# Modulation slabs summed into one PSUM bank, with one copy and one set of folds per layer part

## The chip, the cores and the metric

The kernel runs on one core of a Trainium2 chip. The metric is the device time of one execution in microseconds (us). The kernel before takes 2806.68 us, the median of three runs (2805.99 to 2807.84).

The engines are named as the profile names them: PE (TensorE, matrix products; PEld are its weight loads), DVE (VectorE), ACT (ScalarE), POOL (GpSimd) and SP (SyncE, which here only issues DMAs).

## The reference, cut to what matters

Two layers. In each, a vector `c` of 1024 (and its counterpart `c_ctx` for the context rows) is passed through silu and multiplied by a matrix of 1024 x 6144. The 6144 results are six groups of 1024, by which the activations are shifted, scaled and gated.

```
silu_c = jax.nn.silu(c)
silu_cc = jax.nn.silu(c_ctx)
for i in range(DEPTH):
    mod = (silu_c @ w_ada[i] + b_ada[i])[:, None, :]
    mod_c = silu_cc @ w_ada[i] + b_ada[i]
    sh1, sc1, g1, sh2, sc2, g2 = jnp.split(mod, 6, axis=-1)
    ...
    u = _layer_norm(x) * (1.0 + sc1) + sh1
    uc = _layer_norm(xc) * (1.0 + sc1c) + sh1c
    f, fc = _token_mixer(u, uc, w_in[i], ...)
    x = _post_norm(DEEPNORM_ALPHA * x + g1 * f, ln1_g[i], ln1_b[i])
    u2 = _layer_norm(x) * (1.0 + sc2) + sh2
    ...
    m = _moe(...)
    x = _post_norm(DEEPNORM_ALPHA * x + g2 * m, ln2_g[i], ln2_b[i])
```

The mixer (a state space part with a convolution, a Fourier part and gates) and the mixture of 64 experts are the rest of the kernel. All is float32.

## The kernel before, in words

The kernel is written with explicit engine programs and semaphores. Each engine runs its own list in the order in which the code emits it, and waits where a `wait_ge` says so. No scheduler stands behind it.

**Where the modulation is computed.** The 6144 columns of a layer's `w_ada` come in two parts. The first 2048 (shift and scale of the mixer's input) are four wide slabs of 512 columns. PE works on them at the very start of the kernel for layer 0, and between the experts of layer 0 and the summing of their results for layer 1. The other 4096 are 16 late slabs of 256 columns. They ride in the weight ring of a mixer call (call 0 for layer 0, call 3 for layer 1), one behind each of the call's first 4 + 10 + 2 slabs of `w_in`: the four `four` slabs, the ten `xbc` slabs (convolution channels) and two of the six `z` slabs. The `dt` slab between `four` and `xbc` has 48 columns and no late slab. The ring has four slots. SP loads slab n when the product of slab n - 4 is done.

**A slab's products** (`fourth_products`, L663). `csil` holds silu(c) and silu(c_ctx) as columns 0 and 1 of 32, the other 30 being zero; the contraction of 1024 is 8 steps of 128. Step k writes to partitions 32 (k % 4) onwards, so four partial sums of two rows each lie in four groups of 32 partitions of one bank. ACT copies that bank to SBUF (L1198 wide, L1254 late), with two buffers.

**A fold** (`fold`, L670) brings the sums into the layout in which they are used, one modulation column a partition, and adds the four parts: for each 128 columns of the copy, a matmul with the copy as weights and `fold4` as the moving operand, a constant of 128 x 2 with ones where partition % 32 is 0 or 1. A wide slab needs four such matmuls and a late slab two. PE does the fold of slab n - 1 behind the products of slab n (L690 wide, L791 late), and the last slab's behind the last (L692 wide, L844 late, the latter behind the third `z` slab).

**Use.** DVE adds the bias to the folded sums in one instruction and 1 to the scales in another (`modulate`, L1479), for the wide part in `first_modulations` (L1496) and for the late part after the state passes (L1615). For layer 1, `first_modulations` stands in the middle of DVE's combining of the expert results (L2030), and PE goes from the last wide fold to summing these results (`sum_results`, L643), whose input POOL gathers with plain DMAs (L2116). The second gather waits for the third wide product, the third for the fourth (L2113).

**The xbc loop.** Per slab, PE does 16 matmuls of 256 columns (L747), the late slab's 8 (L667), a fold and four transposes of an older slab (L775). ACT starts the convolution (L1271), DVE does four taps (L1558), ACT the silu (L1238) and the copy of the transposed tile (L1245). Behind the loop DVE waits for ACT's exponentials (L1573) and weights the input of the state products (L1582), which PE awaits at L715.

Each float32 matmul leaves two records in the trace, so x16 there is 8 matmuls.

## Time and profile before

| | |
|---|---|
| time, median of 3 runs | 2806.68 us (2805.99 to 2807.84) |
| profiled execution: span | 2806.5 us |
| its own time | the page gives none beside the span; the median of the runs is 0.2 us above it |
| PE busy | 2563.5 us (91%) |
| DVE / ACT / POOL busy | 962.5 / 543.0 / 238.5 us |
| ACT: copy of a late slab (L1254, 32 of them) | 0.38 us each |
| mean granted clock of PE | 0.957 of full speed |
| late slabs in the trace | 56 to 206 us (layer 0), 1735 to 1890 us (layer 1) |
| wide slabs in the trace | 14 to 40 us (layer 0), 1572 to 1586 us (layer 1) |

The groups of instructions by line give the number of records, the busy time and the mean of one, and behind the bar the engine's idle time just before them with what ended it. The timeline gives start, duration, engine, line and operation, and in brackets the idle time before a row and its releaser, where there was any. A row that merges several instructions runs from the first one's start to the last one's end, so the start of the next row says more on what a step costs than the duration, since matmuls are pipelined.

### The profile page before, as it was taken

Reading aid. Unit: us, or ns where it says so; the run is one execution under the profiler, and the core shown is the slowest. Engines: PE = TensorE matmul, PEld = TensorE weight load, DVE = VectorE, ACT = ScalarE, POOL = GpSimd, SP = SyncE. Lnnn points to the kernel's source line nnn. Section 1 sums busy time; section 2 is a strip of 40 time slices with the busy share of each in tenths; the row PEclk is TensorE's granted clock in tenths of the full one; section 3 lists DMA queues with packets and bytes.
Section 4 is the critical chain, followed back from the end, with each engine's and each line's share of the span. In section 5 each row is a group of like instructions: output and inputs, shape, how many; then the busy total and the mean of one; then the engine's idle time right before and its main releaser. Section 6 shows DMA issues by size and latency. Waiting matters only on the chain. (4 is left out here: it accounts for less than half of the span.)

```text
span 2806.5 us, 35244 instructions
## 1 busy us (share of the span) xinstructions
PE 2563.5 (91%) x11348; PEld 1623.7 (58%) x11348; DVE 962.5 (34%) x2255; ACT 543.0 (19%) x1210; POOL 238.5 (8%) x394
## 2 busy tenths in 40 slices
PE   6999999999997899999999889999997899999994
PEld 3878888887873343433443367878885333434441
DVE  1335724448166111111111375444705311111114
ACT  1233511325131111111111012233411111111110
POOL 0000000000000111112111100000000112112110
PEclk8999999999998999999999989999998999999998
DMA  8764444445335999999999744764441899999993
GB/s 292 237 198 148 158 143 138 135 140 161 120 125 197 410 407 407 408 394 412 408 405 409 295 165 132 227 203 150 147 157 55 343 398 391 390 387 401 381 364 145
DMA packets 293119, 742.43 MB, mean 265 GB/s; under 512 B 33176, under 2 KB 208416, under 8 KB 238240
## 3 DMA queue, kind: packets, MB, share of 16 engines
q1 hardware_dynamic: 264672, 665.59, 63.7%
q0 software_dynamic: 28352, 75.56, 6.9%
q8 instruction: 61, 1.00, 0.1%
q14 instruction: 34, 0.28, 0.0%
HBM read 734.60 MB, written 52.58 MB: 280 GB/s over the span
## 5 line engine op out<-in xcount | busy, mean ns | idle before, releaser
L747 PE MATMUL psum<-arena 128*128 128x256 f32 x1984 | 455.1, 389 | 8.9 <-ACT arena L1212 5.0
L1116 PE MATMUL psum<-arena 128*64 128x512 f32 x1472 | 367.9, 645 | 83.6 <-DMA arena<-in_w 80.6
L747 PEld LDWEIGHTS psum<-arena 128*128 128x128 f32 x1984 | 385.2, 196 | 67.0 <-issue 5.7
L980 PE MATMUL psum<-arena 128*128 128x512 f32 x832 | 374.8, 594 | 0.0
L2004 DVE COPY arena<-psum 128x512 f32<-128x512 f32 x92 | 63.6, 691 | 612.8 <-PE psum L992 308.7
L1116 PEld LDWEIGHTS psum<-arena 128*64 128x64 f32 x1472 | 114.3, 147 | 270.0 <-issue 261.8
L1431 ACT ACTIVATE arena<-psum 128x512 f32<-128x512 f32 x92 | 55.0, 598 | 1057.6 <-PE psum L992 595.3
L758 PE MATMUL psum<-arena 128*128 128x256 f32 (+1 forms) x1088 | 239.6, 379 | 5.0 <-ACT arena L1212 5.0
L980 PEld LDWEIGHTS psum<-arena 128*128 128x128 f32 x832 | 152.2, 192 | 154.3 <-issue 154.3
L758 PEld LDWEIGHTS psum<-arena 128*128 128x128 f32 x1088 | 204.7, 199 | 38.3 <-ACT arena L1212 5.2
L992 PE MATMUL psum<-arena 128*128 128x512 f32 x416 | 198.5, 621 | 12.9 <-DVE arena L1809 9.7
L1558 DVE SCALAR_TENSOR_TENSOR grow<-psum,par,grow 128x255 f32<-128x255 f32 (+1 forms) x304 | 136.2, 479 | 153.9 <-ACT grow L1271 148.4
L907 PE MATMUL psum<-arena 128*128 128x256 f32 x768 | 173.2, 379 | 0.0
L2100 POOL DMA_INDIRECT results<-arena,ids x92 | 93.1, 1012 | 923.8 <-DVE arena L2004 923.8
L1145 PE MATMUL psum<-arena 128*64 128x512 f32 x736 | 168.1, 599 | 0.0
L2001 DVE COPY arena<-psum 128x256 f32<-128x256 f32 x92 | 39.0, 424 | 374.3 <-PE psum L987 374.3
L907 PEld LDWEIGHTS psum<-arena 128*128 128x128 f32 x768 | 144.2, 190 | 23.0
L992 PEld LDWEIGHTS psum<-arena 128*128 128x128 f32 x416 | 77.2, 195 | 128.2 <-issue 115.9
L1102 PEld LDWEIGHTS psum<-cst,arena 128*128 128x128 f32 x736 | 92.8, 193 | 69.4 <-issue 66.9
L2054 POOL MEMSET arena<- 128x1024 f32 x4 | 3.7, 950 | 1378.4 <-DVE arena L1800 1378.4
L1145 PEld LDWEIGHTS psum<-arena 128*64 128x64 f32 x736 | 48.6, 137 | 113.8 <-issue 113.8
L1102 PE MATMUL psum<-cst,arena 128*128 128x128 f32 x736 | 102.7, 283 | 8.6 <-DVEq L1975 4.5
(305 smaller groups left out, 2454.8 us busy)
## 6 DMA issues: line engine op xcount, KB each, us to landing
arena<-in_w SPq DMA_DIRECT2D x414, 1024.0 KB, 14.6
arena<-in_w_in SPq DMA_DIRECT2D x92, 1024.0 KB, 5.3
arena<-in_w_ada SPq DMA_DIRECT2D x32, 1024.0 KB, 7.8
arena<-results POOLq DMA_DIRECT2D x12, 2048.0 KB, 9.5
arena<-in_w_br_ssm SPq DMA_DIRECT2D x24, 768.0 KB, 4.4
arena<-in_w_ada SPq DMA_DIRECT2D x8, 2048.0 KB, 15.3
arena<-cumulated SPq DMA_DIRECT2D x36, 384.0 KB, 4.3
arena<-in_w_br_four SPq DMA_DIRECT2D x12, 1024.0 KB, 5.2
```

The costliest lines, as they stand in the source:

```text
L747: last = mm(o[:, a, :], w[:, k, a * P:(a + 1) * P], rhs[:, k, :], start=k == 0, stop=k == ks - 1, skip_group_check=True)
L758: last = mm(o[:, a, 0:cols], lhs[:, k, a * P:(a + 1) * P], w[:, k, 0:cols], start=k == 0, stop=k == KD - 1, skip_group_check=True)
L907: last = mm(o[:, a, :], w[:, k, a * P:(a + 1) * P], rhs[:, k, :], start=k == 0, stop=k == KD - 1, skip_group_check=True)
L980: last = mm(o.rearrange("p (a n) -> p a n", a=2), lhs(k), w[:, k, :, :], start=k == 0, stop=k == KD - 1)
L992: last = mm(bank[5 + half][:, :], src[:, k, :], w[:, k, half * 512:(half + 1) * 512], start=k == 0, stop=k == 1)
L1102: last = tp(psum[:, 2 + k // 4, (k % 4) * P:(k % 4 + 1) * P], xg[b].rearrange("p (q k) -> p k q", k=KD)[:, k, :], ident)
L1116: last = mm(bank[0][c, :].rearrange("p (a n) -> p a n", a=2), xTe[0][:, k, c], w13[b][:, k, :, :], start=k == 0, stop=k == KD - 1)
L1145: last = mm(bank[5 + half][c, :], hT[0][:, k, c], w2s[b][:, k, half * 512:(half + 1) * 512], start=k == 0, stop=k == 1)
L1431: a_(ysb[b][:, 0:512], bank[5], ACT.Copy).then_inc(z["y_act"], 1)
L1558: i_ = V.scalar_tensor_tensor(dst, src[:, a * SEQ + lo + sh:a * SEQ + hi + sh], par[:, 60 + tap * 20 + ch:61 + tap * 20 + ch], dst, ALU.mu ...
L2004: V.tensor_copy(ysb[b][:, 512:1024], bank[6]).then_inc(z["y_dve"], 1)
L2100: gp.indirect_dma_start(scratch["y"][l], bass.IndirectOffsetOnAxis(ap=ids[:, q:q + 1], axis=0), ysb[b], None, bounds_check=last_row, oob_i ...
```

## The change

- `csil` becomes 62 columns wide with the two silu columns at 30 and 31 and zeros around them. Slab j takes the 32 columns from 2 (15 - j) on, so that its two rows land at rows 2j and 2j + 1 of each group of 32 partitions, and its products add zeros to the other rows.
- All wide slabs of a layer add up in bank 0 and all late slabs in bank 3. Only the very first products of a part start the sum, and only the last ones end it.
- ACT copies the bank once per part, behind the last slab. PE folds once per part, with 8 columns (wide) or all 32 (late) of a wider `fold4`.
- PE no longer waits for ACT's copies between slabs. The second buffer of the copies goes.
- The folded sums now lie with the 128-column block as the outer index and the slab as the inner one, so `modulate` takes one strided addition per block: four for the wide part and two for the late one.
- What is computed, the slabs, their loads and the order of these in SP's queue stay.

```diff
-    pack[:, C_SEL:C_SEL + 2] = (p[:, None] % 32) == np.arange(2)
+    pack[:, C_SEL:C_SEL + 32] = (p[:, None] % 32) == np.arange(32)
...
-        fold4 = cst[:, C_SEL:C_SEL + 2]
+        fold4 = cst[:, C_SEL:C_SEL + 32]
-        csil = sb("csil", [P, KD, 32])
+        csil = sb("csil", [P, KD, 2 * ADA_LATE + 30])
-        late_part = [arena[:, seg_at + b * SW:seg_at + (b + 1) * SW] for b in range(2)]
+        late_part = arena[:, seg_at:seg_at + SW]
-        wide_part = {l: [arena[:, part_at[l] + b * ADA_W:part_at[l] + (b + 1) * ADA_W] for b in range(2)] for l in range(DEPTH)}
+        wide_part = {l: arena[:, part_at[l]:part_at[l] + ADA_W] for l in range(DEPTH)}
...
 
-                def fourth_products(o, w):
-
+                def fourth_products(o, w, j, n):
+
+                    lo = 2 * (ADA_LATE - 1 - j)
                     for k in range(KD):
                         q = 32 * (k % 4)
-                        i_ = mm(o[q:q + 32, :], csil[:, k, :], w[:, k, :], start=k < 4, stop=k >= 4)
+                        i_ = mm(o[q:q + 32, :], csil[:, k, lo:lo + 32], w[:, k, :], start=j == 0 and k < 4, stop=j == n - 1 and k >= 4,
+                                skip_group_check=True)
                     return i_
 
-                def fold(o, part, n):
+                def fold(o, part, n, w):
 
                     for c in range(n):
-                        i_ = mm(o[:, 2 * c:2 * c + 2], part[:, c * P:(c + 1) * P], fold4, start=True, stop=True)
+                        i_ = mm(o[:, w * c:w * (c + 1)], part[:, c * P:(c + 1) * P], fold4[:, 0:w], start=True, stop=True)
                     i_.then_inc(s_ada_tp, 1)
-
-                def wide_fold(j):
-                    pe.wait_ge(s_ada_row, part_no(l, j) + 1)
-                    fold(bank[2][:, 8 * j:8 * j + 8], wide_part[l][j % 2], 4)
 
                 for j in range(ADA_WIDE[l]):
                     r = ADA_RING[l]
                     pe.wait_ge(s_ada[j % r], 16 * (j // r + 1) + 16 * l)
-                    if j >= 2:
-                        pe.wait_ge(s_ada_row, part_no(l, j - 2) + 1)
-                    fourth_products(bank[j % 2], wide[l][j % r]).then_inc(s_ada_mm, 1)
+                    fourth_products(bank[0], wide[l][j % r], j, ADA_WIDE[l]).then_inc(s_ada_mm, 1)
                     if j == 1:
                         pe.wait_ge(s_par, 16 * 7 * (l + 1))
                         tp(bank[7][:, 0:60], praw[0:60, 0, :], ident[0:60, 0:60])
                         tp(bank[7][:, 60:180], praw[0:120, 1, :], ident[0:120, 0:120]).then_inc(s_tp_par, 1)
-                    if j:
-                        wide_fold(j - 1)
-                wide_fold(ADA_WIDE[l] - 1)
+                pe.wait_ge(s_ada_row, 2 * l + 1)
+                fold(bank[2], wide_part[l], ADA_W // P, 2 * ADA_WIDE[l])
                 if l:
                     sum_results(l - 1)
 
...
                         last.then_inc(t_ctp.sem, 1)
 
-                    def late_fold(n):
-                        pe.wait_ge(s_ada_row, late_no(l, n) + 1)
-                        fold(bank[6][:, 4 * n:4 * n + 4], late_part[n % 2], 2)
+                    def late_fold():
+                        pe.wait_ge(s_ada_row, 2 * l + 2)
+                        fold(bank[6], late_part, SW // P, 2 * ADA_LATE)
 
                     def late_ada(kind, j):
                         n = ada_after(m, kind, j)
...
                             return
                         no = SLAB_NO[(m, "ada", n)]
                         pe.wait_ge(s_slab_in[no % NSLOT], 16 * (no // NSLOT + 1))
-                        if n >= 2:
-                            pe.wait_ge(s_ada_row, late_no(l, n) - 1)
-                        fourth_products(bank[3 + n % 2][:, 0:SW], ring[no % NSLOT]).then_inc(s_slab, 1)
-                        if n:
-                            late_fold(n - 1)
+                        fourth_products(bank[3][:, 0:SW], ring[no % NSLOT], n, ADA_LATE).then_inc(s_slab, 1)
 
                     if full:
                         for j in range(4):
@@ -841,7 +823,7 @@
                             late_ada("z", j)
                             state_products(m, True, 3 * j + 2, 3 * j + 3)
                             if m in LATE_CALLS and j == 2:
-                                late_fold(ADA_LATE - 1)
+                                late_fold()
                         scores_product(0)
 
                         def feature_dft(g):
...
             act.wait_ge(s_csil, 1)
             for v in range(2):
-                last = a_(csil[:, :, v], craw[:, v, :], ACT.Silu)
+                last = a_(csil[:, :, 2 * ADA_LATE - 2 + v], craw[:, v, :], ACT.Silu)
             last.then_inc(s_csil, 1)
             for l in range(DEPTH):
                 for j in range(ADA_WIDE[l]):
-                    act.wait_ge(s_ada_mm, wide_no(l, j) + 1)
-                    if j >= 2:
-                        act.wait_ge(s_ada_tp, sums_before(l) + j - 1)
-                    a_(wide_part[l][j % 2], bank[j % 2], ACT.Copy).then_inc(s_ada_row, 1)
+                    if j == ADA_WIDE[l] - 1:
+                        act.wait_ge(s_ada_mm, wide_no(l, j) + 1)
+                        a_(wide_part[l], bank[0], ACT.Copy).then_inc(s_ada_row, 1)
                     if j == 1:
                         act.wait_ge(s_tp_par, l + 1)
...
                     def late_copy(kind, j):
-                        n = ada_after(m, kind, j)
-                        if n is None:
+                        if ada_after(m, kind, j) != ADA_LATE - 1:
                             return
-                        act.wait_ge(s_slab, SLAB_NO[(m, "ada", n)] + 1)
-                        if n >= 2:
-                            act.wait_ge(s_ada_tp, late_no(l, n) - 1)
-                        a_(late_part[n % 2], bank[3 + n % 2][:, 0:SW], ACT.Copy).then_inc(s_ada_row, 1)
+                        act.wait_ge(s_slab, SLAB_NO[(m, "ada", ADA_LATE - 1)] + 1)
+                        a_(late_part, bank[3][:, 0:SW], ACT.Copy).then_inc(s_ada_row, 1)
 
                     if full:
...
                 inverse_root(mv[:, 1:2], 1.0)
                 return V.scalar_tensor_tensor(xres[:, t, :], tmp, rsq[:, 3:4], lnrow[:, 1, :], ALU.mult, ALU.add)
 
-            def modulate(lo, hi, src):
-
-                link(V.tensor_tensor(modc[:, lo:hi, :], src.rearrange("p (j v) -> p j v", v=2),
-                                     par[:, lo:hi].unsqueeze(2).to_broadcast([P, hi - lo, 2]), ALU.add))
+            def modulate(lo, hi, src, wide_by):
+
+                n = (hi - lo) // wide_by
+                for c in range(wide_by):
+                    last = V.tensor_tensor(modc[:, lo + c:hi:wide_by, :], src[:, 2 * n * c:2 * n * (c + 1)].rearrange("p (j v) -> p j v", v=2),
+                                           par[:, lo + c:hi:wide_by].unsqueeze(2).to_broadcast([P, n, 2]), ALU.add)
+                link(last)
                 plain = [o for o in (8, 32) if lo <= o < hi]
...
             def first_modulations(l):
                 dve.wait_ge(s_parc, 2 * l + 2)
-                dve.wait_ge(s_ada_tp, sums_before(l) + ADA_WIDE[l])
+                dve.wait_ge(s_ada_tp, 2 * l + 1)
                 hi = 4 * ADA_WIDE[l]
-                modulate(0, hi, bank[2][:, 0:2 * hi])
+                modulate(0, hi, bank[2][:, 0:2 * hi], ADA_W // P)
                 dve.wait_ge(s_modc, 2 * l + 1)
 
...
                     state_pass(rounds, 0)
 
                     if m in LATE_CALLS:
-                        dve.wait_ge(s_ada_tp, late_no(l, ADA_LATE))
-                        modulate(16, 48, bank[6][:, 0:4 * ADA_LATE])
+                        dve.wait_ge(s_ada_tp, 2 * l + 2)
+                        modulate(16, 48, bank[6][:, 0:4 * ADA_LATE], SW // P)
                         dve.wait_ge(s_modc, 2 * l + 2)
 
 
```

**PE, start of the program (wide slabs of layer 0).** L667 and L659 are the products, L673 and L666 the folds, L688/L689 and L675/L676 transposes of parameters, L721 and L707 the transposes of the normalized input. Before:

```order
L667 MATMUL psum<-arena,csil 32x512 x16
L688 MATMUL psum<-cst,praw 128x60
L689 MATMUL psum<-cst,praw 128x120
L673 MATMUL psum<-cst,arena 128x2 x4
L667 MATMUL psum<-arena,csil 32x512 x8
L673 MATMUL psum<-cst,arena 128x2 x4
L667 MATMUL psum<-arena,csil 32x512 x8
L673 MATMUL psum<-cst,arena 128x2 x8
L721 MATMUL psum<-cst,arena 128x128 x16
```

Of the change, the same place on PE:

```order
L659 MATMUL psum<-arena,csil 32x512 x16
L675 MATMUL psum<-cst,praw 128x60
L676 MATMUL psum<-cst,praw 128x120
L659 MATMUL psum<-arena,csil 32x512 x16
L666 MATMUL psum<-cst,arena 128x8 x4
L707 MATMUL psum<-cst,arena 128x128 x16
```

Sixteen fold matmuls become four, and nothing stands between the products of the last two slabs.

**PE, two turns of the xbc loop (call 0).** L747 and L733 are the slab's matmuls, L667 and L659 the late slab's, L775 and L761 the transposes. Before:

```order
L747 MATMUL psum<-arena 128x256 x16
L667 MATMUL psum<-arena,csil 32x256 x8
L673 MATMUL psum<-cst,arena 128x2 x2
L775 MATMUL psum<-cst,arena 128x128 x4
L747 MATMUL psum<-arena 128x256 x16
L667 MATMUL psum<-arena,csil 32x256 x8
L673 MATMUL psum<-cst,arena 128x2 x2
L775 MATMUL psum<-cst,arena 128x128 x4
```

Of the change, two turns at the same place on PE:

```order
L733 MATMUL psum<-arena 128x256 x16
L659 MATMUL psum<-arena,csil 32x256 x8
L761 MATMUL psum<-cst,arena 128x128 x4
L733 MATMUL psum<-arena 128x256 x16
L659 MATMUL psum<-arena,csil 32x256 x8
L761 MATMUL psum<-cst,arena 128x128 x4
```

The two fold matmuls of each turn are gone, and nothing else changes its place.

## Rows read from the trace of the kernel before

**Rows 1.** The page of the profile: span.
```profile
span 2806.5 us, 35244 instructions
```

**Rows 2.** Timeline of layer 0, two late slabs: start, duration, engine, line.
```profile
56.26 1.07 PE L667 MATMUL psum<-arena,csil 128*32 128x256 f32 x16
57.26 7.17 PE L747 MATMUL psum<-arena 128*128 128x256 f32 x32
...
64.36 1.07 PE L667 MATMUL psum<-arena,csil 128*32 128x256 f32 x16
...
65.36 0.61 PE L673 MATMUL psum<-cst,arena 128*128 128x2 f32 x4
...
65.83 7.15 PE L747 MATMUL psum<-arena 128*128 128x256 f32 x32
```

**Rows 3.** Groups by line, PE, 56.2 to 182 us, then 1734.5 to 1866 us.
```profile
L747 PE MATMUL psum<-arena 128*128 128x256 f32 x417 | 95.6, 388 | 0.0
...
L673 PE MATMUL psum<-cst,arena 128*128 128x2 f32 x52 | 7.9, 256 | 0.0
...
L673 PE MATMUL psum<-cst,arena 128*128 128x2 f32 x52 | 7.9, 257 | 0.0
```

**Rows 4.** Timeline of PE, layer 0, behind the first z slab.
```profile
195.93 0.61 PE L673 MATMUL psum<-cst,arena 128*128 128x2 f32 x4
...
196.40 0.89 PE L715 MATMUL psum<-arena 128*128 128x384 f32 x2
```

**Rows 5.** Timeline of PE and DVE at the xbc loop's end, layer 0.
```profile
167.69 1.07 PE L667 MATMUL psum<-arena,csil 128*32 128x256 f32 x16
...
176.63 1.07 PE L667 MATMUL psum<-arena,csil 128*32 128x256 f32 x16
...
184.79 0.26 DVE L1573 TENSOR_TENSOR arena<-arena 128x96 f32<-128x96 f32 x1 [2.42 <-ACT arena L1290]
...
185.76 1.65 PE L715 MATMUL psum<-arena 128*128 128x384 f32 x2 [2.26 <-DVE arena L1582]
```

**Rows 6.** Timeline of layer 0 behind the last wide slab's products.
```profile
37.71 2.13 PE L673 MATMUL psum<-cst,arena 128*128 128x2 f32 x16
37.83 0.60 ACT L1198 ACTIVATE arena<-psum 128x512 f32<-128x512 f32 x1 [6.27 <-PE psum L667]
...
39.95 0.19 DVE L1481 TENSOR_TENSOR modc<-psum,par 128x32 f32<-128x32 f32 x1 [14.92 <-PE psum L673]
...
46.62 9.71 PE L747 MATMUL psum<-arena 128*128 128x256 f32 x32 [4.96 <-ACT arena L1212]
```

**Rows 7.** Timeline of layer 1, last wide folds and start of the summing.
```profile
1584.41 1.95 PE L673 MATMUL psum<-cst,arena 128*128 128x2 f32 x16
...
1586.17 0.53 POOL L2116 DMA_DIRECT2D arena<-results  x1 [3.63 <-DMA arena<-results]
1586.22 20.85 PE L655 MATMUL psum<-arena 128*128 128x512 f32 x48
...
1596.88 1.28 DVE L2021 TENSOR_TENSOR arena<-arena,psum 128x512 f32<-128x512 f32 x2 [3.64 <-PE psum L655]
```

**Rows 8.** Windows (after ACT and POOL: PEclk), and timeline at the dt products.
```profile
36.00:38.00 2.00, 2.00 (x14) 0.34 (x6) 0.00 (x0) 0.17 (x1) 0.00 (x0) 0.50 1.10 350
90.00:92.00 2.00, 2.00 (x6) 1.55 (x6) 1.72 (x9) 0.00 (x0) 0.00 (x0) 0.50 1.10 355
...
82.93 4.33 PE L758 MATMUL psum<-arena 128*128 128x48 f32 x32
87.07 9.95 PE L747 MATMUL psum<-arena 128*128 128x256 f32 x32
...
1773.02 8.37 PE L747 MATMUL psum<-arena 128*128 128x256 f32 x32
```

**Rows 9.** One line's instructions, L1481 and L667: ns as min/median/max, starts.
```profile
L1481 DVE TENSOR_TENSOR modc<-psum,par x4: 191/203/225, 40.0 to 1899.5; 128x32 f32<-128x32 f32 x2, 128x64 f32<-128x64 f32 x2
...
L667 PEld LDWEIGHTS psum<-arena,csil x640: 105/110/178, 14.2 to 1889.0; 128*32 128x32 f32 x160
```

More of the change, by code:

```diff
@@ L49 @@
 C_SEL = C_TRI8 + NGRP * NGRP
-C_STEP = C_SEL + 2
+C_STEP = C_SEL + 32
 C_FOLD = C_STEP + P
@@ L423, in wide_no @@
             return j + (ADA_WIDE[0] if l else 0)
-        def part_no(l, j):
-            return j + (ADA_WIDE[0] + ADA_LATE if l else 0)
-        def sums_before(l):
-            return ADA_WIDE[0] + ADA_LATE if l else 0
-        def late_no(l, n):
-            return sums_before(l) + ADA_WIDE[l] + n
         @block.sync
```

## The prediction

> **What bounds the kernel now.** I read the page first: one core, span 2806.5 us [rows 1], and TensorE (PE) is busy for most of it. A share of the whole span does not say what an edit is worth in one stretch, so next came the groups of instructions by line over the two stretches in which the late slabs of the modulation run, 56.2 to 182 us (layer 0) and 1734.5 to 1866 us (layer 1) [rows 3]. The reader is to see the last column there: no group of PE has idle time before it, in either stretch. So here PE is the bound, and every instruction that leaves PE's queue moves what follows forward. Third came the timeline of PE, to read what one fold costs in place [rows 2, 4]; fourth the end of the xbc loop, where PE does wait [rows 5]; last the two places where the wide slabs run [rows 6, 7] and the granted clock [rows 8].
>
> **The change part by part**
>
> **Folds inside the late stages (removed).** A late slab without a fold behind it starts its products at 56.26, and the next slab's matmuls start at 57.26: 1.00 us. With a fold pair: 64.36, fold at 65.36, next slab at 65.83 [rows 2]. The products take the same 1.00 us, the pair adds 65.83 - 65.36 = 0.47 us. It costs the same in the z part (195.93 to 196.40) [rows 4]. Each layer has 15 such pairs inside the stage (13 of them in each stretch of rows 3, 52 records at 4 a pair, and 2 among the z slabs), and one behind the stage, which stays.
>
> Of the 15, one saves nothing: the pair behind the last xbc slab. PE's later wait there ends on a chain that starts with the slab product, not with the fold: the product is done at 176.6, VectorE's convolution, ScalarE's exponentials (VectorE waits 2.42 us for them at 184.79) and VectorE's weighting follow, and PE idles 2.26 us before 185.76 [rows 5]. Take the fold out and that pause is 0.47 us longer. So 14 pairs a layer, 28 in all, each 0.47: 28 x 0.47 = -13.2 us. This is the term that carries the forecast.
>
> **The one fold that stays** has 32 columns in place of 2 (8 in place of 2 for the wide slabs). No row shows that form. From below it is the fold of today, 0.47/2 = 0.23 us a matmul; from above the 48-column matmuls of the dt product, 82.93 to 87.07 for 16, 0.26 us each [rows 8]. Two matmuls a layer: 0 to +0.06 us each time. I take 0.
>
> **Copies on ScalarE (removed):** 15 a layer of 0.38 us. ScalarE waits for PE or VectorE in the loop, and in the tail the wait is for VectorE's convolution, which does not wait for the copy. 0 us; at best -0.4 us a layer if the copy is in the chain of rows 5 after all.
>
> **Wide slabs of layer 0.** The folds of slabs 0 to 2 lie between loads that PE waits for, so they are hidden now. At the end the last two folds run back to back from 37.71, and the copy of the last slab (37.83, 0.60 long) is done at 38.43; the second fold starts after the first, at about 38.77 (half of the row's 2.13 us). Afterwards the single fold starts when the copy is done: 0.3 us earlier. The addition on VectorE (39.95) becomes four, each on 8 elements a partition. A row of this line lasts 191 to 225 ns [rows 9], so the three more are 0 to 0.68 us; not chained, they overlap, and I take 0.3. ScalarE and then PE (46.62, after 4.96 us of waiting) hang on this chain [rows 6], so the sum counts: -0.3 + 0.3 = 0, bounds -0.3 to +0.5.
>
> **Wide slabs of layer 1.** Three sets of four folds leave PE, about 1.0 us each, and behind the last products PE waits for the 0.6 us copy. PE would be ready for the summing of results some 2 us earlier than 1586.22. But the gather of the results that it sums landed only then: GpSimd, which waits for the same landing, was released at 1586.17 [rows 7]. So this gain is hidden by a transfer. The second gather is released by the third wide product, about 0.9 us earlier than now, and shares the DMA with the first: the first could land up to 0.9 us later. From 1596.88 on VectorE's chain carries the stage, and it now has the three further additions, +0.3. I take +0.3; bounds -2.0 (the landing is no limit) to +1.6 (0.9 later and 0.68 of VectorE).
>
> **The late modulation** is two additions in place of one, in a stretch in which VectorE waits for PE. 0. The larger zero-padded tile and the 30 further constant columns (15 KB) load while PE waits for the first slabs. 0, at most 0.1.
>
> **Clock of PE.** Behind the dt product of layer 0 the same 16 matmuls take 9.95 us instead of 7.15, with the clock at 1.2 GHz (0.50 in the row of 90 to 92 us); in layer 1 8.37 us [rows 8]. The engine had done 48-column matmuls just before it fell. The fall costs 2.80 and 1.22 us, so the same work can cost either, by how it lies in time, and the change moves it. I take the present sum of the two, 4.0; bounds -2.8 (one gone, the other at 1.2) to +1.6 (both as dear as 2.8).
> The Trainium skill ("TensorE: Matmul & The Clock Gate", section "HAM oscillation") says that bursts of matmuls with waits between them fall back to the slow clock. By that rule this edit has a price: the folds fill pauses in the wide stages, and without them PE is idle more. The trace agrees where PE waits long for a slab: in the row of 36 to 38 us, behind the wait for the last wide one, the clock is 0.50 [rows 8]. By the rule the sum below would be up to 4.4 us higher, the first rival; without it, it stands as it is.
>
> **Sum.** -13.2 + 0 + 0.3 + 0 = -12.9 us. Against the profiled execution: 2806.5 - 12.9 = 2793.6 us. The median of the three runs, 2806.68, is 0.2 above that span, so 2793.8 us. Everything behind the two stages (expert loads included) starts from what PE, VectorE or ScalarE have finished, so I see nothing that takes the gain back.
>
> **Rivals**
>
> 1. **The clock turns against it.** Without the folds PE pauses 0.7 us and more in the layer 1 wide stage, and a fall of the clock lands in the summing of results, which is on the path [rows 7], and the dt product's falls become the dear kind. Price by rows 8: one more fall 2.8, the layer 1 one dearer by 1.6: +4.4, 2798.2 us. For: behind both dt products of these stretches the matmuls are slow [rows 8]. Against: most of the removed work is inside a dense stretch, where it is the fold that is the thin part. Its mirror image is as possible: one dt fall gone and the other cheap (-2.8), and the summing in layer 1 1 us earlier, 2790.0 us.
> 2. **The xbc loop is bound by the convolution, not PE**, and only the folds among the four-slabs and z slabs count: 3 + 2 a layer, 10 x 0.47 = 4.7, 2802 us. For: VectorE and ScalarE work in every xbc turn. Against: no idle time before any PE group [rows 3].
> 3. **Slower: the loads of the shifted slices.** Each load will take its 32 words a partition from an offset that moves by 8 bytes a slab, not from the start of a packed block of 32. The load takes 110 ns now [rows 9], 16 of them in a slab's 1.00 us. If the new pattern makes each 50 ns longer and none of it hides, 32 late slabs cost 32 x 16 x 0.05 = 25.6 us, less 12.9 saved: 2819.4 us. It decides from 25 ns a load (12.9 / 512). For: the offset has no row in this trace. Against: 128 adjacent bytes a partition are read in both, and a slab has time left beside its loads (16 x 0.11 = 1.76 us of them pass in its 1.00 us, so they overlap already).
> 4. **The gain is given back** behind the stage, at a transfer that does not start from PE's progress. I found none; 2800 us if one takes half.
>
> **How the numbers follow.** Forecast as summed 0.68; rival 1 against 0.09 and its mirror image 0.13; rival 2 0.04; rival 3 0.03; rival 4 0.03. The forecast's own bounds, not all at one end, give 2791 to 2797; with the clock's two sides the range is 2789.3 to 2798.5, which leaves out rivals 2 to 4 and the tails of rival 1 and its mirror, under 2 in 10. What a measurement can tell here is 0.2%, 5.6 us. Faster by more: forecast, rival 1 and mirror, rival 4, 0.93; within: rival 2, 0.04; slower: rival 3, 0.03.
>
> **What would show it.** Right: 24 records in place of 192 on the fold's line (2 a matmul, 4 + 2 matmuls a layer); a turn of the xbc loop of 8.47 in place of 8.94 us (167.69 to 176.63) [rows 5]; still no idle before PE's groups in both stretches; the pause before 185.76 of today 2.7 instead of 2.26 us; the summing in layer 1 beginning within 0.1 us of a landing of results, as now. Wrong: a slab's products longer than 1.00 us (rival 3), idle time of PE before the convolution's transposes (rival 2), or the matmuls behind the dt product at a time other than 8.4 to 10 us (the clock).

## The result, and the profile after

The changed kernel takes 2783.7 us in the median of four runs (2783.04 to 2787.53), against 2806.34 us for the kernel before in the same comparison (2798.96 to 2807.84). The ratio is 0.9923, with a 95% interval of 0.9905 to 0.9940: 22.6 us faster. The forecast was 2793.8 us with a range of 2789.3 to 2798.5. The direction was right, the size was not: 1.8 times the forecast gain of 12.9 us, and below the range.

All comparisons below also give means. Runs of one kernel scatter with a standard deviation of some 4 us (the kernel before: 2798.2 to 2814.5 over 50 further runs, mean 2806.4; the changed kernel: mean 2783.8 ± 0.9 over 8), so a single execution can't tell 5 us.

First the page of the changed kernel: the span, and the busy time of each engine.

```profile
span 2781.6 us, 34816 instructions
PE 2529.3 (91%) x11180; PEld 1595.5 (57%) x11180; DVE 963.5 (35%) x2263; ACT 527.9 (19%) x1174; POOL 238.7 (9%) x394
```

The span is 24.9 us shorter than in [rows 1]. Next the groups of PE by line, 46 to 173.5 us, which answer to [rows 3]: records, busy us, mean ns, idle time before them.

```profile
L733 PE MATMUL psum<-arena 128*128 128x256 f32 x448 | 102.0, 387 | 4.1 <-ACT arena L1193 4.1
L659 PE MATMUL psum<-arena,csil 128*32 128x256 f32 x224 | 15.0, 385 | 0.0
L761 PE MATMUL psum<-cst,arena 128*128 128x128 f32 x32 | 5.2, 286 | 0.0
```

The fold's group is gone from the stretch, and PE still idles before none of the loop's groups (the 4.1 us of L733 are before its first matmul at 47.43, outside the stretch of [rows 3]). PE remains the bound. Timeline of PE at two late slabs, to be read beside [rows 2]: start, duration, line.

```profile
56.84 1.07 PE L659 MATMUL psum<-arena,csil 128*32 128x256 f32 x16
57.84 7.17 PE L733 MATMUL psum<-arena 128*128 128x256 f32 x32
64.94 1.07 PE L659 MATMUL psum<-arena,csil 128*32 128x256 f32 x16
65.94 2.42 PE L733 MATMUL psum<-arena 128*128 128x256 f32 x10
```

The next slab's matmuls start 1.00 us behind a late slab's products, every time, with no fold between. The two lines that the change rewrote, durations as min/median/max in ns:

```profile
L659 PEld LDWEIGHTS psum<-arena,csil x640: 105/110/178, 13.3 to 1862.0; 128*32 128x32 f32 x160
L666 PE MATMUL psum<-cst,arena x24: 192/276/379, 37.9 to 1871.8; 128*128 128x8 f32 x16, 128*128 128x32 f32 x8
L1461 DVE TENSOR_TENSOR modc<-psum,par x12: 154/161/192, 39.9 to 1872.2; 128x8 f32<-128x8 f32 x8, 128x32 f32<-128x32 f32 x4
```

The weight loads from the shifted slices take what they took [rows 9], 105/110/178. The folds are 24 records.

What the forecast did not have is at the dt product of layer 0. Timeline of PE there, and two windows (after the busy times of PE, PEld, DVE, ACT and POOL stands PEclk, the granted clock); both answer to [rows 8].

```profile
82.15 3.77 PE L744 MATMUL psum<-arena 128*128 128x48 f32 x32
85.76 7.14 PE L733 MATMUL psum<-arena 128*128 128x256 f32 x32
...
90.00:92.00 2.00, 2.00 (x11) 1.77 (x10) 1.72 (x9) 0.00 (x0) 0.00 (x0) 1.00 1.12 372
86.00:88.00 2.00, 2.00 (x11) 1.74 (x11) 1.55 (x5) 0.28 (x1) 0.00 (x0) 1.00 1.03 343
```

Before, the 48-column product took 4.14 us from its start to the next, and the 32 records behind it 9.87 us to the next line (96.94), with a granted clock of 0.50 (1.2 GHz) for more than half of it. Now it is 3.61 and 7.07 us (to 92.83), at 1.00 (2.4 GHz). So the prediction's own sign of being wrong (these records at a time other than 8.4 to 10 us) is there. It is the same in layer 1, where the row of 32 records took 8.37 us and now takes 7.14:

```profile
1748.10 3.77 PE L744 MATMUL psum<-arena 128*128 128x48 f32 x32
1751.71 7.14 PE L733 MATMUL psum<-arena 128*128 128x256 f32 x32
1758.78 1.07 PE L659 MATMUL psum<-arena,csil 128*32 128x256 f32 x16
```

To see where all of it comes from, I lined up the starts of PE's groups in both traces and noted where the difference changes. Each row is a start before, a start after, and their difference:

| what lies up to there | before | after | difference |
|---|---|---|---|
| first weights of call 0 | 46.62 | 47.43 | +0.8 |
| four slabs, dt product and the 32 records behind it | 98.4 | 93.8 | -4.6 (clock -3.6, folds -1.8, beside the +0.8) |
| rest of the xbc loop, to its last transposes | 178.56 | 170.01 | -8.6 |
| first state products, early z slabs | 206.89 | 196.62 | -10.3 (clock -1.1, folds -0.9) |
| call 1 | 735.38 | 721.12 | -14.3 (clock -1.65 behind its dt product, -1.7 at its end) |
| experts of layer 0 (PE waits for weights), first two wide slabs of layer 1 | 1578.47 | 1561.52 | -17.0 (-0.8 of it clock, in the two slabs) |
| rest of the wide part of layer 1 | 1586.22 | 1568.25 | -18.0 |
| summing of the results, to the dt product of call 2 | 1636.79 | 1620.21 | -16.6 |
| call 2, and call 3 to the 32 records behind its dt product | 1782.79 | 1759.78 | -23.0 (folds -1.8, clock -1.7 at this dt product and -1.8 in call 2, where a pause is 1.1 shorter too) |
| late stage of layer 1 | 1862.47 | 1835.47 | -27.0 |
| end | | | -24.9 |

The folds show as 28 steps of 0.44 to 0.45 us (a turn of the xbc loop is 168.52 - 160.02 = 8.50, before 8.94 [rows 5]). That is 12.5 us. The rest, half of the gain, sits in other steps, and the largest that can be read one by one are those of the clock. The wide part of layer 1 does not carry it in this profile: the 1.0 us that it gains is gone when the summing ends.

Timeline of PE at the end of the xbc loop, which answers to [rows 5]:

```profile
168.52 1.07 PE L659 MATMUL psum<-arena,csil 128*32 128x256 f32 x16
169.52 0.66 PE L761 MATMUL psum<-cst,arena 128*128 128x128 f32 x4
...
174.76 0.30 PE L685 MATMUL psum<-cst,arena 128*32 128x128 f32 x1 [1.09 <-ACT arena L1226]
...
177.66 0.94 PE L701 MATMUL psum<-arena 128*128 128x384 f32 x2 [2.27 <-DVE arena L1563]
```

From the last late products to the first state product it is 9.14 us (168.52 to 177.66) and was 9.13 (176.63 to 185.76): the fold behind the last xbc slab saved nothing, as forecast, but the time it leaves appears ahead of the transposes at 174.76 and not in the last pause, which stays 2.27.

### The profile page after: what moved, and what is told of

Its sections match the earlier page's. It is cut to its first block and busy times, and to the rows that moved or that the text cites. A ratio compares the mean times of both kernels' runs of the same rounds, so it can differ in the third digit from the quotient of the medians.

```text
span 2781.6 us, 34816 instructions
## 1 busy us (share of the span) xinstructions
PE 2529.3 (91%) x11180; PEld 1595.5 (57%) x11180; DVE 963.5 (35%) x2263; ACT 527.9 (19%) x1174; POOL 238.7 (9%) x394
## 5 line engine op out<-in xcount | busy, mean ns | idle before, releaser
L733 PE MATMUL psum<-arena 128*128 128x256 f32 x1984 | 447.7, 385 | 6.9 <-ACT arena L1193 4.1
L1098 PE MATMUL psum<-arena 128*64 128x512 f32 x1472 | 361.2, 635 | 90.0 <-DMA arena<-in_w 88.2
L733 PEld LDWEIGHTS psum<-arena 128*128 128x128 f32 x1984 | 379.4, 193 | 66.4 <-issue 7.6
L974 PE MATMUL psum<-arena 128*128 128x512 f32 x416 | 198.5, 621 | 12.9 <-DVE arena L1790 9.7
L889 PE MATMUL psum<-arena 128*128 128x256 f32 x768 | 173.2, 379 | 0.0
L1127 PE MATMUL psum<-arena 128*64 128x512 f32 x736 | 168.1, 598 | 0.0
```

The lines of the kernel that those rows point to most:

```text
L733: last = mm(o[:, a, :], w[:, k, a * P:(a + 1) * P], rhs[:, k, :], start=k == 0, stop=k == ks - 1, skip_group_check=True)
L889: last = mm(o[:, a, :], w[:, k, a * P:(a + 1) * P], rhs[:, k, :], start=k == 0, stop=k == KD - 1, skip_group_check=True)
L974: last = mm(bank[5 + half][:, :], src[:, k, :], w[:, k, half * 512:(half + 1) * 512], start=k == 0, stop=k == 1)
L1098: last = mm(bank[0][c, :].rearrange("p (a n) -> p a n", a=2), xTe[0][:, k, c], w13[b][:, k, :, :], start=k == 0, stop=k == KD - 1)
L1127: last = mm(bank[5 + half][c, :], hT[0][:, k, c], w2s[b][:, k, half * 512:(half + 1) * 512], start=k == 0, stop=k == 1)
```

## The experiments

The columns: median, mean with its standard error, ratio to the kernel before on the same chip with 95% interval, and the time that TensorE's clock stood at 0.50 in the mixer stretches (60 to 810 and 1560 to 2090 us) of the one profiled execution.

| kernel | median | mean (runs) | ratio, interval | at 1.2 GHz |
|---|---|---|---|---|
| before | 2806.6 | 2806.4 ± 0.5 (50) | | 75 us |
| changed | 2783.7 | 2784.5 ± 1.0 (4) | 0.9923, 0.9905 to 0.9940 | 45 |
| changed, again | 2782.5 | 2783.2 ± 1.7 (4) | 0.9926, 0.9909 to 0.9943 | 48 |
| late_only | 2786.7 | 2787.0 ± 0.8 (4) | 0.9942, 0.9925 to 0.9958 | 48 |
| wide_only | 2800.9 | 2800.6 ± 1.2 (10) | 0.9986, 0.9975 to 0.9998 | 65 |
| refold | 2802.7 | 2802.3 ± 1.6 (10) | 0.9992, 0.9977 to 1.0007 | 58 |
| pair_at_dt | 2786.5 | 2784.8 ± 1.3 (5) | 0.9920, 0.9904 to 0.9936 | 51 |
| pairs_but_dt | 2796.3 | 2796.6 ± 2.1 (5) | 0.9957, 0.9941 to 0.9974 | 61 |
| wide_refold | 2784.6 | 2785.1 ± 0.8 (5) | 0.9921, 0.9906 to 0.9936 | 51 |
| fill | 2775.2 | 2775.9 ± 1.7 (4) | 0.9888, 0.9869 to 0.9908 | 31 |
| fill_before | 2798.3 | 2798.0 ± 0.8 (9) | 0.9970, 0.9958 to 0.9981 | 58 |
| hold_before | 2800.3 | 2799.9 ± 0.8 (12) | 0.9977, 0.9967 to 0.9987 | 34 |
| hold_wide | 2796.2 | 2796.7 ± 0.8 (8) | 0.9965, 0.9951 to 0.9978 | 31 |
| hold_after | 2786.7 | 2786.0 ± 0.9 (6) | 0.9930, 0.9915 to 0.9946 | 32 |

The last column is one execution each. The mean granted clock is on record for every execution, and since the traces show only the levels 0.50 and 1.00, twice what it lacks of 1, times the span, is an estimate of the time at 1.2 GHz in the whole execution: 234 ± 2 us before (50 executions), 212 ± 2 in the changed kernel (8), 228 ± 5 in `refold` (10), 203 ± 6 in `fill` (4), 212 ± 4 in `fill_before` (9), 188 ± 2 in `hold_before` (12), 199 ± 2 in `hold_after` (6). A microsecond at half speed costs at most 0.5, and less where TensorE waits. So the 21 us by which the changed kernel stands at 1.2 GHz for less time are worth up to 11 us, about what its gain has beside the folds.

### The changed kernel once more

No edit.

> The changed kernel again, beside the kernel before. Theory A (the folds give 28 x 0.45 = 12.5 us, and the other 10 to 12 us are falls of PE's clock that a shift in time happened to take away): the difference to before need not be the same on another chip or day, 2780 to 2792. Theory B (the other 10 us are work or waits that the change takes away, the same each time): 2783 to 2784 in every run.

Mean 2783.2 us, and again no fall of the clock behind the dt products of the two calls with late slabs. The extra gain is no accident of one comparison.

### The late part alone, the wide part alone

`late_only` has the shifted slices, one copy and one fold set for the 16 late slabs; the wide slabs are folded as before. `wide_only` is the reverse.

```
 late_only:  fourth_products(bank[j % 2], wide[l][j % r], 0, 1)      # wide slabs, each by itself
             fold(bank[2][:, 8 * j:8 * j + 8], wide_part[l][j % 2], 4, 2)
 wide_only:  fourth_products(bank[3 + n % 2][:, 0:SW], ring[no % NSLOT], 0, 1)   # late slabs, each by itself
             fold(bank[6][:, 4 * n:4 * n + 4], late_part[n % 2], 2, 2)
```

> Late slabs as in the change, wide slabs as before. Folds of the late part: 28 x 0.45 = 12.5 us less. Theory A: 2794 from the folds alone, and up to 10 us less where falls of the clock go with the shift; which falls go is read from the granted clock in the trace. Theory B, with the rest coming from the wide part: 2794, and wide_only then gives the other 10 us.

> Wide slabs as in the change, late slabs as before. By the steps of the prediction +0.3 us, 2806.6. Theory A: within 2 us of before, apart from falls of the clock that come or go. Theory B, with the rest from the wide part: 2796.

Against the mean before on that chip (2805.7), the late part gives 18.7 ± 1.2 us, though its folds are worth 12.5; the wide part gives 5.1 ± 1.5, forecast as nothing. With the late part alone the clock falls behind neither of these dt products. Timeline of PE of `late_only`, layer 0:

```profile
80.97 3.77 PE L760 MATMUL psum<-arena 128*128 128x48 f32 x32
84.58 7.14 PE L749 MATMUL psum<-arena 128*128 128x256 f32 x32
```

### The pairs of folds put back, without their waits

```
+                        if n:
+                            for c in range(2):
+                                mm(bank[6][:, 64 + 2 * c:66 + 2 * c], cst[:, c * P:(c + 1) * P], fold4[:, 0:2], start=True, stop=True)
```

The changed kernel with 15 pairs of matmuls a layer in the old form and place; they read a constant, wait for no copy, and nobody reads them.

> The change, with two fold matmuls put back behind each late slab from the second on (15 pairs a layer; they read a constant, wait for nothing and are not used). Copies and waits stay away. Theory A: PE's time is back, +12.5 us, and with it the old places in time: 2796 to 2808, with falls of the clock behind the dt products again. Theory B (copies, waits or the one bank gave the rest): 2796, with no more falls than in the changed kernel.

It costs 18.5 ± 1.9 us against the changed kernel's mean of 2783.8, where 30 pairs at 0.45 are 13.4, and 12.5 without the two behind the last xbc slabs, which fall into a pause. So the pairs as PE work alone, without copies or semaphores, take away more than their own duration. Timeline of PE of `refold` in layer 0; compare 3.77 in the changed kernel:

```profile
82.68 0.61 PE L777 MATMUL psum<-cst 128*128 128x2 f32 x4
83.14 4.78 PE L744 MATMUL psum<-arena 128*128 128x48 f32 x32
```

The product after the pair runs 4.58 us to the next line (87.72) instead of 3.61.

### Is it the pair beside the dt product?

The same three lines under `if n == 3:` (only the pair ahead of the dt product, one a layer) and under `if n and n != 3:` (all the others).

> The changed kernel with one fold pair put back per layer, behind the late slab that stands directly ahead of the dt product (it reads a constant and is not used). Theory A (thin work next to the dt product brings PE's clock down, and this pair tips it): the clock falls behind the dt product again, +3.3 us in layer 0 and +1.7 in layer 1 beside the pair's own 0.9: 2789.5. Theory B (a fall or none is where the dt product happens to lie in time): the pair costs its own 0.9 us, 2784.5, and any fall comes with about the chance it has elsewhere.

> The changed kernel with all pairs put back but the one of pair_at_dt (14 a layer). Theory A: no fall behind the dt products, 28 x 0.45 = 12.5 us more than the change: 2796. Theory B: 12.5 us and in addition falls as often as in the kernel with all 15, whose mean was 2802.4: 2801.

`pair_at_dt` costs 1.0 ± 1.6 us over the changed kernel; two pairs are 0.9 by themselves. In layer 0 the clock stays up with the pair in place, in layer 1 it falls. `pairs_but_dt` costs 12.8 ± 2.3, close to 28 x 0.45 = 12.6, although its profiled execution shows slow stretches behind both dt products without a pair ahead of them. Timelines of PE in layer 0, `pair_at_dt`, then `pairs_but_dt`:

```profile
83.53 0.61 PE L777 MATMUL psum<-cst 128*128 128x2 f32 x4
83.99 3.75 PE L744 MATMUL psum<-arena 128*128 128x48 f32 x32
```

```profile
81.29 4.06 PE L744 MATMUL psum<-arena 128*128 128x48 f32 x32
85.15 7.05 PE L733 MATMUL psum<-arena 128*128 128x256 f32 x25
```

The last row is cut off at the end of the window; the 32 records take 8.49 us to the next line (93.64).

So the simple theory, that the pair directly ahead of the 48-column product alone tips the clock, falls. In the one profiled execution of `pairs_but_dt` the falls are back without that pair, though its mean shows no cost beyond the pairs' own time. The two runs also show how far one profile and the mean can stand apart.

All profiles without fillers in the dt products, taken together, say more than any one of them. At the dt products of calls 0 and 3, the calls with late slabs, the clock falls in 7 of 8 cases with all pairs in place (`before`, `wide_only`, `refold`, `fill_before`), in both of `pairs_but_dt`, in one of two of `pair_at_dt`, and in 1 of 10 without pairs (the changed kernel twice, `late_only`, `wide_refold`, `fill`). Call 1 has no late slab, so nothing of the change is in it; there the clock falls in 4 of the 11 profiles (`before`, `pairs_but_dt`, `fill`, `fill_before`). In call 2 the whole dt product runs at 0.50 in all 11.

### Is the wide part's gain its folds?

```
+                    if j:
+                        for c in range(4):
+                            mm(bank[2][:, 64 + 2 * c:66 + 2 * c], cst[:, c * P:(c + 1) * P], fold4[:, 0:2], start=True, stop=True)
```

The changed kernel with the 12 wide folds a layer put back as dead work.

> The changed kernel with the three sets of four fold matmuls put back between the products of the wide slabs (they read a constant, wait for nothing and are not used). The two kernels with only the wide part changed or not changed say that the wide part gives 3 to 4.5 us in the mean. Theory A (PE's fold work ahead of the summing in layer 1 is what went): half or more of it comes back, 2785.5 to 2788. Theory B (the waits for the copies, or a changed load at the start): nothing comes back, 2783.8.

Mean 2785.1: +1.3 ± 1.2 us. That is within the error of nothing, and at most a part of the 3 to 5 us.

### Holding the clock up

`fill` is the changed kernel with matmuls that nobody reads, placed in pauses of PE: ahead of call 0's first product, and around the `heads_product` ahead of the state products.

```
+            def fill(o, n, cols):
+                for _ in range(n):
+                    mm(o[:, 0:cols], ident, cst[:, 0:cols], start=True, stop=True)
...
+                        if m == 0:
+                            fill(bank[1], 3, 512)
...
+                            if full:
+                                fill(bank[4], 2, 256)
                             if full:
                                 heads_product(m)
+                                fill(bank[4], 2, 512)
```

> The changed kernel with matmuls of a constant, not used, in PE's pauses: 3 of 512 columns while ScalarE writes the first u of layer 0, and 2 of 256 and 2 of 512 columns before the first state product of each call with all parts. If pauses are what lets the clock fall there, the long slow stretch at 35 to 52 us ends one step earlier (-1.7 us) and the three falls of 3.4 to 6.8 us ahead of the state products go (-1.7 to -3.4 each): 2776 to 2780. If not, or if the fillers come in the way, 2784 to 2786.

It is the fastest kernel of the study: mean 2775.9, 7.9 ± 1.9 us under the changed kernel. Its profile still has a fall of 3.4 us behind each dt product of layer 0 (83.1 to 86.5 in call 0, 455.2 to 458.6 in call 1). Timeline of PE of `fill`, layer 0, to be held against the rows of the changed kernel above:

```profile
174.35 1.98 PE L652 MATMUL psum<-cst 128*128 128x512 f32 x4
176.69 0.91 PE L708 MATMUL psum<-arena 128*128 128x384 f32 x2 [0.35 <-DVE arena L1572]
177.44 2.32 PE L753 MATMUL psum<-arena 128*128 128x256 f32 x10
```

PE's pause of 2.27 us is filled. From the last late products (167.55) to the state product it is 9.14 us, as in the changed kernel, and the ten records behind it take 2.15 us to the next line. In the changed kernel they took 3.84:

```profile
178.41 4.01 PE L744 MATMUL psum<-arena 128*128 128x256 f32 x10
182.25 0.81 PE L701 MATMUL psum<-arena 128*128 128x384 f32 x2
```

### The change measured again with the clock held

Four kernels test the cause: nearly the same fillers in the kernel before (`fill_before`, with bank 6 in place of bank 4 and four matmuls of 256 columns in place of two of 512), and in addition fillers inside the dt product of every call, in the kernel before (`hold_before`), in the wide part alone (`hold_wide`) and in the changed kernel (`hold_after`).

```
+                    def refill(done):
+                        if done % 8 == 0:
+                            fill(bank[6][:, 256:512], 3, 256)
-                    token_major("dt", 0, uT, 48)
+                    token_major("dt", 0, uT, 48, refill)
```

The dt product is 16 matmuls or 32 records; the fillers are 2 x 3 matmuls a call, which are 12 records of 0.223 us. The expectation of `hold_before` counts these records as matmuls, and the fall that it lists at 731 us is at the end of call 1 and not behind a dt product. That of `hold_after` overlooks the second fall in layer 0 of `fill`.

> The kernel before with the same filler matmuls as in the run 'fill' (3 of 512 columns while TensorE waits for the first transposed copies of call 0; 2 of 256 before and 4 of 256 after the heads product at the first state product of each full call; results never read). Theory C (the clock is the second half of the gain): the filler takes away the falls before the state products and leaves those behind the dt products, because the pairs of fold matmuls and the 48-column matmuls still stand there: 2806.9 - 8 = about 2799, and the difference to 'fill' (2775.9 in the mean) stays 20 to 25. Rival D (what the change gains beside the folds' own time is waits of the pairs and copies, not the clock): also 2799 and also 20 to 25; this run does not tell them apart by itself, it is the lower rung of 'hold_before'.

> As 'fill_before', and 3 filler matmuls of 256 columns behind every 8 of the 32 matmuls of each call's dt product (12 a call, 4 calls, 48 by 0.223 = 10.7 us of added TensorE time). Theory C: the falls behind the dt products (before: 85.9, 468, 731 and 1772 us; 3.3, 1.65, 1.7 and 1.7 us in the alignment of the traces) go, so it costs 10.7 - 8.3 = 2.4 over 'fill_before': about 2801, and it stands 12.5 to 15 above 'hold_after'. Rival D: the fillers only add, 10.7 over 'fill_before' (2810), and the difference to 'hold_after' stays 20 to 25.

> The wide part of the change alone (the slabs of the first modulation gathered in one bank, one copy, one set of folds per layer; the late part as before), with the same filler matmuls as 'hold_before'. Theory C: what 'wide_only' gained (5 us) was mostly the clock, so this stands 0 to 1.5 below 'hold_before'. Rival E (the wide part saves waits of TensorE or start loads whatever the clock does): 3 to 5 below 'hold_before'.

> The changed kernel with the same filler matmuls as 'hold_before'. 'fill' had no fall left behind the dt products of layer 1 and one of 3.4 us in layer 0, so the 10.7 us buy nearly nothing: 2775.9 + 10.7 - 1 = about 2786. Theory C: the difference hold_before - hold_after is the folds' own time, 28 pairs by 0.45 = 12.5, and up to 2.5 more. Rival D: 20 to 25 as between the kernels without filler.

The means are 2798.0, 2799.9, 2796.7 and 2786.0.

- With fillers at the starts only, the change is worth 22.1 ± 1.9 us (2798.0 - 2775.9), as without.
- The fillers in the dt products are 10.7 us of work in either kernel. In the changed one they cost 10.1 ± 1.9. In the kernel before they cost 1.9 ± 1.1: the other 8.8 us are slow clock that goes away. The granted clock of all executions agrees: the time at 1.2 GHz falls by 24 ± 5 us from `fill_before` to `hold_before`, which is worth up to 12 us, and by 4 ± 6 from `fill` to `hold_after`.
- With them the change is worth 13.9 ± 1.2 us. The late part is 10.7 ± 1.2 of it, the wide part 3.2 ± 1.1. The clock is not held alike in every stretch, though: by the estimate above `hold_after` stands 10 ± 3 us longer at 1.2 GHz than `hold_before`, so the change without any clock could be worth up to 5 us more than 13.9.

Timeline of PE of `hold_before`, layer 0: the fold pair is there, the 48-column product is there, and the 32 records take 7.00 us to the next line.

```profile
80.90 0.61 PE L677 MATMUL psum<-cst,arena 128*128 128x2 f32 x4
81.37 1.96 PE L767 MATMUL psum<-arena 128*128 128x48 f32 x16
83.17 1.53 PE L661 MATMUL psum<-cst 128*128 128x256 f32 x6
84.54 1.88 PE L767 MATMUL psum<-arena 128*128 128x48 f32 x16
86.25 1.53 PE L661 MATMUL psum<-cst 128*128 128x256 f32 x6
87.62 7.07 PE L756 MATMUL psum<-arena 128*128 128x256 f32 x32
```

Between the profiles of `hold_wide` and `hold_after` the folds show as clean steps of 0.44 or 0.45 us, and the dt products of calls 0, 1 and 3 add nothing: 12.8 us up to the last transposes of the xbc loop of layer 1 (1851.43 and 1838.61), of which 0.4 lies ahead of call 0's first weights.

The wide part, for which I had expected a remainder of 0 to 1.5, keeps 3.2. One place where it shows is layer 1. Timelines of PE, first `hold_before`, then `hold_wide`, from the second pair of wide slabs to the summing of the results:

```profile
1570.54 0.96 PE L677 MATMUL psum<-cst,arena 128*128 128x2 f32 x8
1571.43 1.93 PE L671 MATMUL psum<-arena,csil 128*32 128x512 f32 x16
1573.28 1.05 PE L677 MATMUL psum<-cst,arena 128*128 128x2 f32 x8
1574.26 1.92 PE L671 MATMUL psum<-arena,csil 128*32 128x512 f32 x16
1576.12 1.95 PE L677 MATMUL psum<-cst,arena 128*128 128x2 f32 x16
1577.93 12.26 PE L655 MATMUL psum<-arena 128*128 128x512 f32 x28
```

```profile
1570.00 3.64 PE L672 MATMUL psum<-arena,csil 128*32 128x512 f32 x32
1574.36 1.06 PE L679 MATMUL psum<-cst,arena 128*128 128x8 f32 x8 [0.72 <-ACT arena L1205]
1575.27 15.27 PE L655 MATMUL psum<-arena 128*128 128x512 f32 x35
```

7.39 us from the folds' first row to the summing become 5.27 from the corresponding products: 2.1 us less, and PE does not wait for a landing at the start. But it waits for landings inside the summing, and when the dt product of call 2 starts (1628.51 and 1627.54) only 0.3 of it is left, counted from the parameter transposes. In call 2 it comes up again: PE's pause there is 2.95 us in place of 4.39, and the 32 records behind it take 8.66 in place of 9.80 at a slow clock. So how much of the 3.2 us is the wide part's own and how much the clock is not shown.

## Why the prediction was wrong, by its steps

1. **The folds inside the late stages: right.** 28 steps of 0.445 us, 12.5 in place of 13.2, since a turn without the pair is shorter by 0.44 and not by 0.47. The one behind the last xbc slab saves nothing, as said.
2. **The clock: the step that failed.** I wrote that the change moves the falls behind the dt products and took "the present sum of the two, 4.0", so a term of 0 with -2.8 as the best end. Measured, the fillers in the dt products take 8.2 ± 2.2 us off the change's worth (22.1 - 13.9): so much of its gain was clock around them. Three things were wrong in it. I counted two falls; the alignment shows one behind the dt product of call 1 too (-1.65). I priced only the matmuls behind the product and not the product itself (4.14 to 3.61 in layer 0, 4.03 to 3.61 in layer 1), so these two places give 3.3 and 1.7 us. And I took the falls as random in place, when the pairs were part of what made them likely: 7 of 8 with all pairs, 1 of 10 without; with wide matmuls laid into the dt product they went while the pairs stayed (`hold_before`). Outside the dt products the clock gave something too, which my term did not have: 1.1 us at the first state products of layer 0 and 1.7 at the end of call 1 in these two profiles.
3. **The wide part of layer 1: about right in this profile, for another reason, and not settled in the mean.** I took +0.3, with -2.0 as the end at which the landing of the results is no limit. At the start of the summing the changed kernel is 1.0 us earlier, after a wait for a landing; in `hold_wide`, which doesn't wait there, 2.0. The timeline of the changed kernel, which answers to [rows 7]:

```profile
1560.48 0.57 POOL L2097 DMA_DIRECT2D arena<-results  x1 [5.84 <-issue]
...
1561.97 3.64 PE L659 MATMUL psum<-arena,csil 128*32 128x512 f32 x32
...
1566.33 1.06 PE L666 MATMUL psum<-cst,arena 128*128 128x8 f32 x8 [0.72 <-ACT arena L1179]
1568.25 20.84 PE L646 MATMUL psum<-arena 128*128 128x512 f32 x48 [0.87 <-DMA arena<-results]
1568.64 0.53 POOL L2097 DMA_DIRECT2D arena<-results  x1 [3.86 <-DMA arena<-results]
```

   I had taken the first gather's landing as fixed or later. Its issue waits for the stores of the expert results and not for PE's wide products, and came 16.1 us earlier (1560.48, before 1576.54); PE waited for its landing until 1568.25, 7.8 us after the issue. Before, PE started at 1586.22, 9.7 after it. Why it landed sooner, though the second gather followed sooner too, is not shown. But the 1.0 us does not last: the summing waits 1.20 and 2.13 us where it waited 0.93 and 1.00, and from the parameter transposes to the dt product of call 2 it is 58.7 us (1561.52 to 1620.21), before 58.3 (1578.47 to 1636.79), so +0.4. The same stretch takes 56.5 to 58.7 us in the profiles with the new wide part and 58.3 to 60.1 in those with the old one.
4. **The wide part of layer 0: right in the chain, and swamped by the clock in this profile.** The fold starts at 37.91, when the copy is done, and the four additions take 0.38 us, but they start only 0.05 us earlier than before (39.90, 39.95), and PE's first weights stand 0.8 us later. The clock was 0.50 at 40 to 42 us where it had been 1.00, and the transposes on the way to ACT took 3.65 us in place of 1.95:

```profile
39.65 3.65 PE L707 MATMUL psum<-cst,arena 128*128 128x128 f32 x16
...
39.90 0.38 DVE L1461 TENSOR_TENSOR modc<-psum,par 128x8 f32<-128x8 f32 x4 [15.87 <-PE psum L666]
...
41.69 5.69 ACT L1193 ACTIVATE arena<-psum,modc 128x128 f32<-128x128 f32 x16 [3.83 <-PE psum L707]
47.43 0.80 PE L733 MATMUL psum<-arena 128*128 128x256 f32 x1 [4.13 <-ACT arena L1193]
```

   That would be the first rival's mechanism (PE idle more in the wide stage, the clock slower), but it is one profile: in `wide_only` and in the second profile of the changed kernel the transposes take 1.94 us and PE's pause is 4.97 and 4.96, as before. In `wide_only` it is 11.83 us from the last slab's products to the first weights (34.25 to 46.08), before 12.22 (34.40 to 46.62), so 0.4 less where the clock is alike.
5. **Copies, late modulation, shifted slices: nothing, as said.** The rivals of a convolution-bound loop and of slower loads are excluded by the groups without idle time and by the 105/110/178 ns. The fourth, a gain given back behind the stage, did not come for the late part; the 1.0 us of the wide part was given back in the summing.

**What the Trainium skill says of it.** "TensorE: Matmul & The Clock Gate", section "HAM oscillation", speaks of bursts of matmuls with waits between. I used it against this change, since it takes PE work out. The runs show the other side: in `refold` PE was busier, and the clock in the mixer stretches stood at 1.2 GHz for 58 us, in the two profiles of the changed kernel for 45 and 48. The falls behind the dt products of calls 0, 1 and 3 come with no wait of PE just ahead of them, so they are not that section's case.

**What stays open.** What makes the clock fall in a given execution isn't settled: `pair_at_dt` and `pairs_but_dt` show that neither the neighbouring pair nor the others decide alone, and executions of one kernel differ by 4 us either way. Where the wide part's 3.2 ± 1.1 us lie is seen only in part: 0.3 to 0.6 in each wide stage, the rest in call 2, mixed with the clock. The waits for landings in the summing differ from profile to profile. How the 8.2 us (± 2.2) divide over the four dt products was read from single profiles only, and the fall at the end of call 1, gone in the changed kernel, is back in the profiles of `hold_after` and `late_only`, so it is not tied to the folds.

## What to carry to other kernels

Where the trace shows the granted clock at half speed behind a stretch of narrow matmuls, price that as part of the edit: taking other thin matmuls out of the same dense stretch can be worth more than their duration, here 18.7 us for 12.5 us of folds (`late_only`). To find what an edit is worth by itself, measure both kernels again with wide matmuls that nobody reads laid into the thin stretches; the difference of the two pairs is the clock's share. Check with the granted clock of all executions that it really is held alike in both. And a few such matmuls in a pause that PE has anyway, ahead of a dense stretch, can pay: here they gave another 7.9 us, though three such places were filled at once and not tried one by one.

## What the runs showed of the hardware

- The 16 matmuls of 48 columns at a stretch are followed by a granted clock of 0.50 in some executions (before: 90 to 92 us) and 1.00 in others (changed: the same window), although PE has no idle time there; with 6 matmuls of 256 columns laid among them the clock was 1.00 behind the dt products of calls 0, 1 and 3 in the profiles of `hold_before`, `hold_wide` and `hold_after`, at 1.9 us net in the kernel before and 10.1 in the changed one. In call 2, where the product starts at 0.50 after a wait of 4.96 us, it was 1.00 before its end.
- A matmul with 2 moving columns took 0.22 us in place (0.445 a pair), close to the 0.23 of one with 48 columns in the same stage (3.61 us for 16), and about half of one with 256 (7.07 for 16): between 48 and 2 columns next to nothing is saved here.
- 32 weight columns read from a slice that moves by 8 bytes a slab load in the same 105/110/178 ns as from a fixed block.
